# Second block's modulation weights as whole slabs beside the down pass, two jobs per group

## The reference, cut to what matters

```
# second block, per layer i
c_act = silu(c_2)
shift, scale, gate = split(c_act @ ada_w_2[i] + ada_b_2[i], 3)
kv_shift, kv_scale = split(c_act @ kv_ada_w_2 + kv_ada_b_2, 2)

# end of the first block, beside which it is computed
gt, up = split(h2 @ w_gu, 2)                       # 2816 features each
x = x + g2 * ((silu(gt) * up) @ w_down)
```

## Time and profile before

| | us |
|---|---|
| median of three runs | 2913.84 (2913.36 to 2915.66) |
| profiled execution | 2912.8, its span 2911.0 |
| PE busy | 2818.2 (97%) |
| DVE busy | 1878.1 (65%) |
| ACT busy | 1103.3 (38%) |
| POOL busy | 404.8 (14%) |
| granted PE clock, mean | 0.987 of full |

### The profile page before, as it was taken

One profiled execution on the slowest core, in us unless ns is written; L12 is line 12 of the kernel. 1 busy time (PEld: TensorE's weight loads), 2 busy tenths in 40 slices (PEclk: granted clock), 3 DMA queues, 4 the chain that ended last, 5 costly groups with the idle time before them and its releaser, 6 DMA issues.

```text
span 2911.0 us, 40919 instructions
## 1 busy us (share of the span) xinstructions
PE 2818.2 (97%) x16244; PEld 2229.3 (77%) x16244; DVE 1878.1 (65%) x2269; ACT 1103.3 (38%) x1499; POOL 404.8 (14%) x444
## 2 busy tenths in 40 slices
PE   5998999999899999999999999999999999999999
PEld 4886567778778888788777888888788887777777
DVE  6557738762887776577478748567868345455463
ACT  4124446652433333221244424334434125444462
POOL 3012010001100000121102112021212002222240
PEclk8999999999999999999899999999999999999999
DMA  7454011011154442655114233243521321212121
GB/s 246 145 166 112 6 30 31 18 36 44 46 150 135 144 133 81 203 174 172 44 58 143 79 99 105 73 138 124 171 89 58 116 88 51 73 37 73 37 88 58
DMA packets 272905, 281.92 MB, mean 97 GB/s; under 512 B 16160, under 2 KB 236497, under 8 KB 272737
## 3 DMA queue, kind: packets, MB, share of 16 engines
q1 hardware_dynamic: 212848, 190.20, 21.1%
q0 software_dynamic: 13888, 42.41, 5.1%
q10 hardware_dynamic: 46000, 46.94, 4.8%
HBM read 234.95 MB, written 42.18 MB: 95 GB/s over the span
## 4 chain that ended last, share of the span: by engine, by line
PE 87%; DVE 5%; ACT 4%; issue 2%; DMA 1%; SPq 1%; POOL 0%; ACTq 0%; DVEq 0%; POOLq 0%
PE PU L1192 13%; PE PU L1194 13%; PE PU L1193 13%; PE PM L1704 4%; PE PM L1705 4%; PE PM L1706 4%; PE PM L1966 3%; PE PM L1978 2%; PE PU L1954 2%; PE PU L1208 2%; PE PM L1998 2%; PE PU L1582 2%; PE PM L2000 2%; PE PU L1209 2%; PE PU L1210 2%; PE PM L1999 2%
## 5 line engine op out<-in xcount | busy, mean ns | idle before, releaser
L1192 PE MATMUL PU<-hH,w_hi_t 128*128 128x512 f32 (+1 forms) x1440 | 568.7, 395 | 0.9 <-DVE w_lo_t L2883 0.6
L1194 PE MATMUL PU<-hH,w_lo_t 128*128 128x512 f32 (+1 forms) x1440 | 561.3, 390 | 0.0
L1193 PE MATMUL PU<-hL,w_hi_t 128*128 128x512 f32 (+1 forms) x1440 | 560.8, 389 | 0.0
L1192 PEld LDWEIGHTS PU<-hH,w_hi_t 128*128 128x128 f32 (+1 forms) x1440 | 269.2, 187 | 58.5 <-issue 1.7
L1194 PEld LDWEIGHTS PU<-hH,w_lo_t 128*128 128x128 f32 (+1 forms) x1440 | 269.0, 187 | 58.7
L1193 PEld LDWEIGHTS PU<-hL,w_hi_t 128*128 128x128 f32 (+1 forms) x1440 | 269.4, 187 | 55.0
L2112 ACT ACTIVATE w_hi_t<-w_raw 128x1024 fp32r<-128x1024 f32 x125 | 131.3, 1050 | 417.0 <-PE PU L1194 313.1
L3908 DVE TENSOR_TENSOR_SCAN s_keep<-s_keep,zero 128x128 f32<-128x128 f32 (+7 forms) x128 | 181.9, 1422 | 76.3 <-POOL s_keep L1148 76.3
L2883 DVE TENSOR_TENSOR w_lo_t<-w_raw,w_hi_t 128x1024 fp32r<-128x1024 f32 x139 | 185.8, 1336 | 63.2 <-ACT w_hi_t L2112 55.1
L3416 DVE SCALAR_TENSOR_TENSOR xT<-PU,mod,xT 128x1024 f32<-128x1024 f32 x80 | 102.6, 1282 | 153.5 <-PE PU L1194 153.1
L1148 POOL TENSOR_SCALAR_AFFINE_SELECT s_keep<-s_keep 128x128 f32<-128x128 f32 x128 | 94.4, 744 | 464.2 <-ACT s_keep L2769 463.9
(11 more groups left out here) (576 smaller groups left out, 5871.5 us busy)
## 6 DMA issues: line engine op xcount, KB each, us to landing
w_raw<-in_m_in_w_dram SPq DMA_DIRECT2D x40, 512.0 KB, 3.9
gu_rows<-in_w_gu_dram ACTq DMA_DIRECT2D x36, 512.0 KB, 5.0
ada_w<-in_w_ada_dram POOLq DMA_DIRECT2D x32, 512.0 KB, 4.7
seg<-decay_sums SPq DMA_DIRECT2D x32, 512.0 KB, 4.0
ada_half<-in_ada_w_dram SPq DMA_DIRECT2D x64, 192.0 KB, 2.3
ada_late<-in_ada_w_dram POOLq DMA_DIRECT2D x32, 384.0 KB, 3.6
w_raw<-in_w_down_dram SPq DMA_DIRECT2D x22, 512.0 KB, 5.1
gated_tiles<-f_out ACTq DMA_DIRECT2D x20, 512.0 KB, 3.1
```

The lines of the kernel that those rows point to most:

```text
L1192: mm(PU[0:width, up, half, :], whi, aH[:, k, cols], start=k == 0, stop=False)
L1193: mm(PU[0:width, up, half, :], whi, aL[:, k, cols], start=False, stop=False)
L1194: last = mm(PU[0:width, up, half, :], wlo, aH[:, k, cols], start=False, stop=k == kt - 1)
```

## The change

The half slabs go, with their loads, buffers, DVE steps and column sums in the block products; so PE runs all five passes in its loop. All eight jobs run beside the down pass as whole slabs by GpSimd's queue: in groups 0 to 3 DVE takes two slabs behind each evacuation (k = 0 and 1, 2 and 3, and so on), a job takes four units, and two jobs a group. Buffers stay two. PE's column sums stand behind unit 5 of the group for its first job and behind unit 1 of the next group for its second, the bias sums behind panels 2 and 0.

```diff
-HALF_AT = {0: 0, 2: 1, 3: 2, 5: 3, 6: 4, 8: 5, 9: 6, 11: 7}
...
-            slab = Tally(4 * KD)
-
-            def half_slabs(i, l):
-
-                for k in range(KD):
-                    if k == 1:
-                        sp.wait_ge(ada_acc_s, ADA_JOBS + 2 * i + l)
-                    else:
-                        sp.wait_ge(ada_used, slab(-1))
-                    dst = ada_half[:, k % 2, :]
-                    sp.dma_start(dst[:, 0:384], ada2[:, l, k, bass.ds(3 * P * i, 3 * P)]).then_inc(half_landed[k % 2], 16)
-                    sp.dma_start(dst[:, 384:512], kva[:, k, bass.ds(2 * P * i + l * P, P)]).then_inc(half_landed[k % 2], 16)
-                    slab.next()
...
-            with counted(sp, 4, [(slab, 2 * KD)]) as i:
-                for l in range(2):
-                    half_slabs(i, l)
...
-            sp.wait_ge(ada_acc_s, ADA_JOBS + 8)
             sp.wait_ge(f_gated, F_GATED + 2 * (F_PAIRS - 1))
...
-            slab.n += 8 * KD
             g.wait_ge(gu_done, GU_DONE + 7 * (F_PAIRS - 1) + 4)
-            for i in range(4, 8):
+            for i in range(8):
                 for k in range(KD):
                     g.wait_ge(ada_used, slab(-1))
                     dst = ada_late[:, k % 2, :]
...
-            def phases_body(i, jobs):
+            def phases_body(i):
 
                 for r in range(4):
                     for q in range(7):
                         phase(i, r, q)
-                    if jobs and r % 2:
-                        ada_columns(4, half_columns)
-
-            with counted(pe, 4, [(job, 2)]) as i:
-                phases_body(i, 1)
-            phases_body(4, 0)
+
+            with pe.Fori(0, F_PAIRS // 4) as i:
+                phases_body(i)
...
-                        if (c, u) == (0, 1) and 0 < g < 5:
+                        if (c, u) == (0, 1) and 0 < g < 5 or (c, u) == (2, 1) and g < 4:
                             ada_columns()
...
-                def half_slab(p):
-
-                    k = HALF_AT.get(p % 14)
-                    if jobs and k is not None:
-                        ada_slab(ada_half[:, k % 2, :], ada_half_acc[:, :], ada_half[:, 1, :], cact[:, 8:16], k, half_landed, 2 * KD - 1)
...
-                    half_slab(7 * r)
...
-                    if jobs and r % 2:
-                        l = r // 2
-                        ada_finish([(48 + 24 * l + 3 * i, 128 + 24 * l + 3 * i, 3), (96 + l + 2 * i, 176 + l + 2 * i, 1)], half_columns)
-
-            with counted(ve, 4, [(slab, 2 * KD), (job, 2), (reduced, 2), (ch, 2)]) as i:
-                lows_body(i, 1)
-            lows_body(4, 0, last=True)
+            with counted(ve, 4, [(ch, 0)]) as i:
+                lows_body(i)
+            lows_body(4, last=True)
             tiles_low(0, range(2, 4))
             ve.wait_ge(gu_done, GU_DONE + 7 * F_PAIRS)
+            def modulation(n):
+
+                ada_finish([(48 + 3 * n, 128 + 3 * n, 3), (72 + 3 * n, 152 + 3 * n, 3), (96 + 2 * n, 176 + 2 * n, 2)])
+
             for g in range(D_GROUPS - 1):
                 for c in range(4):
                     split()
                     for t in (2 * c, 2 * c + 1):
                         evacuated("g2", t)
                         if g < 4:
-                            ada_slab(ada_late[:, t % 2, :], ada_late_acc[:, 0, :], ada_late_acc[:, 1, :], cact[:, 8:16], t, ada_landed, 4 * KD)
+                            for k in (2 * t % KD, 2 * t % KD + 1):
+                                ada_slab(ada_late[:, k % 2, :], ada_late_acc[:, 0, :], ada_late_acc[:, 1, :], cact[:, 8:16], k)
                     if c == 1:
                         tiles_low(g + 1, range(min(4, FT - 4 * g - 4)))
-                        if g:
-                            n = 3 + g
-                            ada_finish([(48 + 3 * n, 128 + 3 * n, 3), (72 + 3 * n, 152 + 3 * n, 3), (96 + 2 * n, 176 + 2 * n, 2)])
+                    if c == 0 and g:
+                        modulation(2 * g - 1)
+                    if c == 2 and g < 4:
+                        modulation(2 * g)
             ve.wait_ge(rp_landed, 16 * 12)
             for hd in range(2):
                 r = slice(hd * HD, (hd + 1) * HD)
```

More of the change, by code:

```diff
@@ L365, in two_blocks @@
         gu_lo = [at(f"gu_lo{b}", 12288 + 1024 * b + 512, [P, 4, P], F32R) for b in range(F_SLOTS)]
-        ada_half = at("ada_half", 8192, [P, 2, 512])
-        ada_half_acc = at("ada_half_acc", 9216, [P, 512])
         gu_mid = at("gu_mid", 9728, [P, 2, 512])
@@ L511, in two_blocks @@
         x_landed = [sem(f"x_pair_landed{t}_then_gated_tiles_loaded{t}") for t in range(2)]
-        x_landed += [sem(f"x_pair_landed{t + 2}_then_half_slab_landed{t}") for t in range(2)]
-        f_landed, half_landed = x_landed[0:2], x_landed[2:4]
+        x_landed += [sem(f"x_pair_landed{t + 2}") for t in range(2)]
+        f_landed = x_landed[0:2]
         x_t = sem("x_tile_transposed")
@@ L1707, in phase @@
                 last.then_inc(gu_done, 1)
-            def half_columns(s):
-                return PU[:, s, 0, 0:4]
-            def phases_body(i, jobs):
+            def phases_body(i):
                 for r in range(4):
@@ L3503, in tiles_low, with lows_body @@
                     V.tensor_tensor(low[:, k, :], raw[:, k, :], high[:, k, :].bitcast(F32), ALU.subtract).then_inc(f_act, 1)
-            def half_columns(s):
-                return PU[:, s, 0, :]
-            def lows_body(i, jobs, last=False):
+            def lows_body(i, last=False):
                 tt = V.tensor_tensor
                 f1, f2 = f_out[:, 0:512], f_out[:, 512:T]
-                def half_slab(p):
-                    k = HALF_AT.get(p % 14)
-                    if jobs and k is not None:
-                        ada_slab(ada_half[:, k % 2, :], ada_half_acc[:, :], ada_half[:, 1, :], cact[:, 8:16], k, half_landed, 2 * KD - 1)
                 for r in range(4):
@@ L3535, in lows_body @@
                         weight_sum(i, r + 1, 3)
-                    half_slab(7 * r + 1)
                     ve.wait_ge(gu_done, done + 3)
@@ L3543, in lows_body @@
                         weight_sum(i, r + 1, 4)
-                    half_slab(7 * r + 2)
                     ve.wait_ge(gu_done, done + 4)
@@ L3549, in lows_body @@
                         phase_low(i, r + 1, 0)
-                        half_slab(7 * r + 3)
                         phase_low(i, r + 1, 1)
-                        half_slab(7 * r + 4)
                     else:
@@ L3561, in lows_body @@
                         phase_low(i, r + 1, 2)
-                        half_slab(7 * r + 5)
                     else:
@@ L3571, in lows_body @@
                         phase_low(i, r + 1, 3)
-                        half_slab(7 * r + 6)
                     ve.wait_ge(gu_gated, GU_GATED + 4 * i + r + 1)
```

## The result

The changed kernel takes 2980.34 us (2976.95 to 2983.13, four runs) against 2914.75 us for the kernel before on the same chips, a ratio of 1.0226 with a 95% interval of 1.0209 to 1.0242: **65.6 us slower**. The forecast was 2953 and 2930 to 2978. The direction and the mechanism were right, the size was not: the measured loss is 66 us, the forecast one 40, and the time lies 2 us above the range, where rival D (landings above 5 us throughout) was placed.

What follows compares the result with a forecast made beforehand. PE bounds the kernel, with 87% of the chain that ended last. Block products -3.2, down-pass refill waits +32, panel contention +8 and gated tiles +3 gave +40 us on 2912.8: 2953, eight in ten 2930 to 2978.

Steps and rivals of the forecast that it cites:

- rival D: Slab loads: more in flight delay one another, landings above 5 us throughout; +66 and more, 2979 to 3000; chance 0.06.
- Block products, -3.2: Block-product loop: eight column sums of about 0.4 us leave PE, minus 3.2 us; the DVE and SP work removed is worth 0.
- The sum of DVE's work, 43.1 us a group: Down pass: DVE's work in a group sums to 43.1 us, which by itself just fits under PE's 44.4.
- Refill of 4.5 us: Down pass: a slab buffer is full 4.5 us after its read, 5.8 after its slab began, against a 5.44 us unit.
- The walk through a group, 52.9 us: Down pass, groups 1 to 3: steps between units' first slabs sum to 52.9 us against 43.9, 9.0 us lost a group.
- steps 3 to 4 and 7 to 0: Down-pass group: DVE's own work sets these steps, 11.9 and 7.4 us; refill called hidden in the first.
- Group 0, 5 us: Down pass, group 0: DVE starts on time, first loss at unit 6, 2.6 us plus 2.2 for the lower clock, together 5.
- Contention, 8 for panels and 3 for gated tiles: Down pass: slab loads meeting panel loads cost 8 us, those behind gated tiles 3 us, at most 14.
- the step 4 to 5: Down-pass group, first slab of a job: DVE's work 3.2 us, refill 5.2; the step takes 5.2.
- The upper bound, 2979: Whole kernel: every landing at 5.0 us adds 1.5 to each of six refill-bound steps; net +66, 2979.
- Rival B: Down pass: refills hide, only the pile-up between units 3 and 4 shows; +6, 2919, up to 2928; chance 0.08.
- Rival C: Down pass: not slower, DVE's 43.1 us fit under 44.4, only column sums count; -1.6, 2911; chance 0.03.

Runs made afterwards that it cites:

- e7: Changed kernel with modulation jobs 0 to 3 left out, jobs 4 to 7 placed as in the kernel before; 2912.8 us, ratio 0.9989.
- e1: Changed kernel with all slab loads left out but the first two of 64, all slab work kept; 2930.14 us, ratio 1.0053.
- e2: Changed kernel with four slab buffers instead of two, bytes and order unchanged; 2932.97 us, ratio 1.0062.
- e12: Changed kernel with both DMAs per slab kept, each moving an eighth of the columns from the third slab on; 2935.24 us, ratio 1.0063.
- e10: Changed kernel with gated tiles of groups 1 to 5 and down panels of groups 1 to 3 cut to 32 columns; 2962.09 us, ratio 1.0157.
- e4: Changed kernel with down panels of groups 1 to 3 loaded in 32 of 256 columns per row tile; 2976.17 us, ratio 1.0208.
- e3: Changed kernel with gated tiles of groups 1 to 5 loaded in 32 of 1024 columns; 2967.3 us, ratio 1.0179.
- e9: Changed kernel with four slab buffers and the next group's low halves one each behind evacuations 3 to 6; 2913.61 us, ratio 0.9990.
- e6: Changed kernel with the second DMA of each slab (128 KB) dropped from the third slab on; 2963.15 us, ratio 1.0160.
- e5: Changed kernel with four slab buffers, slabs spread over 36 units, low halves one each behind evacuations 3 to 6; 2916.3 us, ratio 1.0001.

## Why the prediction missed

Two terms of the sum were too small: the walk through a group without contention, 48 us where the sum had 32, and contention, 18 to 20 where it had 11. By its own steps:

**Block products, -3.2: right.** -3.2 in the trace, -3.3 in e7. (A column sum, four products in the code, stands as eight small matmuls in the trace, the x8 of the earlier trace rows; its price was read from the distance and holds.)

**The sum of DVE's work, 43.1 us a group: right** (43.2 and 43.1 in the windows above), and so was that it does not decide alone (e1).

**Refill of 4.5 us, with the slab's own time 5.8 and longer than the unit's 5.44: right as a mechanism.** e1, e2 and e12 show that it decides: without refills, with buffers to hide them, or with refills of 3.0 us, 47 to 50 of 66 us go.

**The walk through a group, 52.9 us: too short, and this is the step that failed.** I took one wait a step, that of the pair's first slab, and wrote "refill hidden" at steps 3 to 4 and 7 to 0. The changed kernel's DVE in group 1:

```profile
1263.24 0.74 DVE L2888 TENSOR_SCALAR ada_late_acc<-ada_late,cact 128x1024 f32<-128x1024 f32 x1
1264.09 1.29 DVE L2891 SCALAR_TENSOR_TENSOR ada_late_acc<-ada_late,cact,ada_late_acc 128x1024 f32<-128x1024 f32 x1
1265.29 1.28 DVE L3386 SCALAR_TENSOR_TENSOR xT<-PU,mod,xT 128x1024 f32<-128x1024 f32 x1
1268.65 1.28 DVE L2891 SCALAR_TENSOR_TENSOR ada_late_acc<-ada_late,cact,ada_late_acc 128x1024 f32<-128x1024 f32 x1 [2.08 <-DMA ada_late<-in_kv_ada_w_dram]
1270.57 1.28 DVE L2891 SCALAR_TENSOR_TENSOR ada_late_acc<-ada_late,cact,ada_late_acc 128x1024 f32<-128x1024 f32 x1 [0.64 <-DMA ada_late<-in_kv_ada_w_dram]
...
1274.30 1.28 DVE L2891 SCALAR_TENSOR_TENSOR ada_late_acc<-ada_late,cact,ada_late_acc 128x1024 f32<-128x1024 f32 x1
1277.62 1.29 DVE L2891 SCALAR_TENSOR_TENSOR ada_late_acc<-ada_late,cact,ada_late_acc 128x1024 f32<-128x1024 f32 x1 [2.04 <-DMA ada_late<-in_kv_ada_w_dram]
...
1280.32 1.28 DVE L2891 SCALAR_TENSOR_TENSOR ada_late_acc<-ada_late,cact,ada_late_acc 128x1024 f32<-128x1024 f32 x1 [0.22 <-DMA ada_late<-in_kv_ada_w_dram]
1283.32 1.28 DVE L2891 SCALAR_TENSOR_TENSOR ada_late_acc<-ada_late,cact,ada_late_acc 128x1024 f32<-128x1024 f32 x1 [1.72 <-DMA ada_late<-in_kv_ada_w_dram]
1284.64 1.25 DVE L2880 STREAM_TRANSPOSE ada_late_acc<-ada_late_acc 128x1024 f32<-128x1024 f32 x1
1285.92 1.22 DVE L2881 TENSOR_REDUCE ada_red<-ada_late_acc 128x32 f32<-128x1024 f32 x1
1287.06 4.62 DVE L3473 TENSOR_TENSOR hL<-hL,hH 128x1024 fp32r<-128x1024 f32 x4
1291.60 1.22 DVE L2853 TENSOR_TENSOR w_lo_t<-w_raw,w_hi_t 128x1024 fp32r<-128x1024 f32 x1
1292.73 1.28 DVE L3386 SCALAR_TENSOR_TENSOR xT<-PU,mod,xT 128x1024 f32<-128x1024 f32 x1
1293.92 0.74 DVE L2888 TENSOR_SCALAR ada_late_acc<-ada_late,cact 128x1024 f32<-128x1024 f32 x1
```

Behind the first slab of a unit the second waits too (1270.57, 1277.62, 1283.32), and the second slab of units 3 and 7 stands in front of the transpose and the reduce, so its wait comes on top of a step that has no slack. From first slab to first slab the steps are 5.4, 5.7, 6.0 and then 13.6 (1280.32 to 1293.92), where I had 5.2, 5.8, 5.8 and 11.9. So the second slab's waits behind units 0 to 2 cost next to nothing where they stand, because the first slab's refill sets those steps. But they put the second buffer further and further behind, and the bill comes at unit 3: its 1.72 us are the 1.7 that the step is too long. That the second is late has two causes, both to be seen in GpSimd's queue for the pair behind 1263.24:

```profile
1264.28 0.71 POOL L1065 DMA_DIRECT2D ada_late<-in_ada_w_dram  x1 [4.25 <-DVE ada_late_acc L2888]
1264.98 0.56 POOL L1067 DMA_DIRECT2D ada_late<-in_kv_ada_w_dram  x1
1265.67 0.71 POOL L1065 DMA_DIRECT2D ada_late<-in_ada_w_dram  x1
1266.38 0.57 POOL L1067 DMA_DIRECT2D ada_late<-in_kv_ada_w_dram  x1
```

The second load is issued 1.4 us behind the first, and with both in flight it lands 4.2 us after its second part's issue (1266.38 to 1270.57), not 3.5: in the change's trace second loads issued 1.3 to 2.2 us behind the first take 3.7 to 5.0. I had priced every load by the median of a kernel in which loads are seldom in flight together. In e10, where the other loads of these groups are cut to an eighth or less, the group comes to 56.7 to 57.9 in place of 52.9, 14 us over groups 1 to 3. Of these, 11 us lie in the steps 3 to 4 and 7 to 0, and the waits of their second slabs sum to 11.0; the six other steps together are 0.5 to 1.5 us too long in a group.

**Group 0, 5 us: too small as well.** I let DVE be on time up to unit 6; its pairs wait from unit 1 on, and in e10 the group takes 55.7 for 44.1, a loss of 11.5. My own walk, applied from unit 1 on, would have given 9 for this group too; the rest is the second slabs again. Group 4 gives some 2 us back (39.1 for 41.2 from its first evacuation to group 5's, since its own is late), which I had at nothing. Together the part without contention is 45.3 + 3.2 = 48 us where the sum had 32: **16 of the 26 us that are missing.** (The groups of e10's trace add up to 18, 2 more than the times do.)

**Contention, 8 for panels and 3 for gated tiles: the sizes were the wrong way round and the sum too small.** e4 gives 4, e3 gives 13, together 18 to 20 for 11: **the other 9.** Which step of a group meets the gated tiles was wrong where it cost most. In group 0, and then in group 1: SP's issue, the wait of DVE that it brought, and the landing (second parts issued at 1234.20 and 1309.88):

```profile
1231.84 1.88 SPq L792 DMA_DIRECT2D hL<-gated_tiles  x4
...
1242.73 1.28 DVE L2891 SCALAR_TENSOR_TENSOR ada_late_acc<-ada_late,cact,ada_late_acc 128x1024 f32<-128x1024 f32 x1 [6.95 <-DMA ada_late<-in_kv_ada_w_dram]
...
DMA to landing us min/median/max: 8.5/8.5/8.5
...
1307.83 2.01 SPq L792 DMA_DIRECT2D hL<-gated_tiles  x4
...
1317.62 1.28 DVE L2891 SCALAR_TENSOR_TENSOR ada_late_acc<-ada_late,cact,ada_late_acc 128x1024 f32<-128x1024 f32 x1 [3.61 <-DMA ada_late<-in_kv_ada_w_dram]
...
DMA to landing us min/median/max: 7.7/7.7/7.7
```

In group 0 the tiles meet the loads of unit 5's slabs, in the step 4 to 5: it takes 10.3 us where I had 5.2, and 5.2 in e3. In group 1 four tiles are issued at 1307.83, when PE has finished unit 7 of the group. I took the slabs of unit 7 to be there by then, so that the tiles would fall on the refills behind them, in the step to the next group with its 1.6 us of slack. But DVE took the slabs of unit 6 as late as 1305.3 and 1307.6, so the loads of unit 7's slabs were issued at 1306.84 and 1309.18 and met the tiles themselves: waits of 2.66 and 3.61 us in front of the job's last two slabs, which have no slack at all.

**Bounds and chances.** The upper bound, 2979, was made with landings of 5.0 throughout and came out by its number, not by its reason: the median landing was 3.7, and rival D did not happen either. What lies outside my range is first the wait of the second slab behind units 3 and 7 of each group, which the walk did not have, and then the gated tiles, which I had put at 3 us though "at most 14" stood beside it. Rival B is what e1 and e2 show once the refill is hidden, +15 to +18 where it was put at +6 to +15 (2919 to 2928): its stalls are 2.4 us instead of 1.9 (2.6 in my own term for group 0) and bring the lower clock in two of four cases in e1, in four of four in e2. Rival C is excluded by the same runs: a second slab behind unit 3 is too much for the order even with every load there, and e9 shows that this was the order and not the amount.

Where the Trainium skill's fit for a transfer (DMA: Bandwidth & Descriptors, the anatomy of one SWDGE DMA) was set against the rows, its fixed part of about 2.0 us agrees with e12's landing of 2.0; it is the part with the bytes that is larger here. Sharing the way with the 384 KB issued 0.7 us before does not explain it alone, for in e6 the 384 KB land only after 3.8 us with no second part behind them; why is not shown.

## What to carry to other kernels

When loads move to a stage where they follow one another closely, compare the whole refill (last reader's end, issue, landing) with the time until the buffer is wanted again, and walk through every load of the round, not the first of each pair: a late load makes the next load of the same buffer later, and the bill comes where a long chain hangs on the last one. Price a landing in the company that it will have, from rows where two are in flight. And ask first what the stage that is to be relieved can give: here 3 us, which four buffers and low halves taken one by one would have kept (e9), and which two buffers in the plain order turned into a loss of 66.

## What the runs showed of the hardware beside

A stall of PE of 2.40 us was followed by matmuls at full clock twice and by six to eight at the lower level (0.43 us apart) twice, in one and the same execution (e1). In e2 four stalls (three of 2.4 us, one of 4.4) all had the lower level behind them within 1.3 us of PE's restart. A stall of 1.82 us kept the full clock (changed kernel, 1248.15) and one of 1.83 us did not (e5, above). So by these rows the length of a stall of about 2 us does not tell which level follows. In the changed kernel, with a stall of 5 to 7 us in each group, the mean clock of groups 1 and 2 is 0.89. With the pair of loads in flight together the second one's landing is up to 1.5 us above the median of 3.5 of the kernel before; with 2 MB of gated tiles in front the longest landings of groups 0 to 2 are 7.7 to 8.6 us, and 7.1 with 1 MB in group 3.
